# Three buffers for the split weights, modulation chunks in the mixers' room, an earlier first low half, and ten filler products for sixteen

## The reference, cut to what matters

```python
def swiglu(h, w_gate, w_up, w_down):
    return (jax.nn.silu(h @ w_gate) * (h @ w_up)) @ w_down
...
    cond = jax.nn.silu(c)
    for l in range(DEPTH):
        mod = (cond @ mod_w[l] + mod_b[l]).reshape(B, 9, D)
        h = modulate(rmsnorm_2(x, norm_g[l, 0]), mod[:, 0], mod[:, 1])
        x = x + 0.5 * mod[:, 2][:, None, :] * swiglu_2(h, ffn_w1[l, 0], ffn_w2[l, 0])
        h = modulate(rmsnorm_2(x, norm_g[l, 1]), mod[:, 3], mod[:, 4])
...
        x = x + mod[:, 5][:, None, :] * y
        h = modulate(rmsnorm_2(x, norm_g[l, 2]), mod[:, 6], mod[:, 7])
        x = x + 0.5 * mod[:, 8][:, None, :] * swiglu_2(h, ffn_w1[l, 1], ffn_w2[l, 1])
    return rmsnorm_2(x, final_norm_g)
```

## Time and profile before

| | us |
|---|---|
| median of 3 runs | 2264.15 (2263.81 to 2268.41) |
| the profiled execution, its own time | 2260.51 |
| its span in the trace | 2258.7 |
| PE busy in it | 2152.3 (95%) |
| DVE busy | 1611.8 (71%) |
| ACT busy | 1199.0 (53%) |

### The profile page before, as it was taken

How to read it: one execution, slowest core, us unless ns; L and a number is a source line. 1 busy time by engine, 2 the same in 40 slices (tenths; PEclk the granted TensorE clock), 3 DMA queues, 4 the chain that set the end, 5 groups by cost and what they waited for, 6 DMA issues and landing times.

```text
span 2258.7 us, 32271 instructions
## 1 busy us (share of the span) xinstructions
PE 2152.3 (95%) x12896; PEld 1852.2 (82%) x12896; DVE 1611.8 (71%) x2638; ACT 1199.0 (53%) x2024; POOL 41.8 (2%) x38
## 2 busy tenths in 40 slices
PE   8999978999999997999989999899999999999998
PEld 7888957888888895888878888688888888658887
DVE  7887486887787648688678767578776656786665
ACT  6554555554554455555465546555455544455553
POOL 0002000000001100000000000000000000000000
PEclk9999989999999998999999999899999999799999
DMA  7876412777577641277757764167755454103544
GB/s 271 290 262 224 167 56 88 257 254 247 208 262 263 224 164 46 103 260 245 258 176 260 241 222 148 61 208 260 239 188 186 174 197 137 69 1 131 186 170 147
DMA packets 78072, 426.29 MB, mean 189 GB/s; under 512 B 9696, under 2 KB 10464, under 8 KB 47632
## 3 DMA queue, kind: packets, MB, share of 16 engines
q1 hardware_dynamic: 77968, 424.95, 54.6%
HBM read 423.86 MB, written 1.05 MB: 188 GB/s over the span
## 4 chain that ended last, share of the span: by engine, by line
PE 73%; DVE 15%; DMA 6%; ACT 5%; issue 1%; DVEq 0%; ACTq 0%
PE bank L418 34%; PE bank L415 17%; DVE slot_lo L1162 6%; DMA slot<-in_wd_dram 5%; PE bank L408 4%; PE bank L410 4%; PE bank L409 4%; ACT slot_hi L848 2%; DMA slot<-in_slots_dram 2%; DVE h L1212 1%; PE bank L761 1%; PE bank L563 1%; PE bank L455 1%; DVE room L1434 1%; PE bank L475 1%
## 5 line engine op out<-in xcount | busy, mean ns | idle before, releaser
L1162 DVE TENSOR_TENSOR slot_lo<-slot,slot_hi 128x1024 fp32r<-128x1024 f32 (+1 forms) x728 | 799.2, 1113 | 279.2 <-ACT slot_hi L848 278.0
L418 PE MATMUL bank<-h_both,slot_hi 128*128 128x512 f32 x2816 | 970.6, 398 | 10.4 <-DVE slot_lo L1162 6.6
L848 ACT ACTIVATE slot_hi<-slot 128x1024 fp32r<-128x1024 f32 (+1 forms) x728 | 678.3, 957 | 268.0 <-PE bank L418 90.2
L415 PE MATMUL bank<-h_both,slot_lo 128*128 128x256 f32 x2816 | 734.3, 281 | 0.0
L418 PEld LDWEIGHTS bank<-h_both,slot_hi 128*128 128x128 f32 x2816 | 506.9, 188 | 111.2 <-issue 12.6
L415 PEld LDWEIGHTS bank<-h_both,slot_lo 128*128 128x128 f32 x2816 | 531.6, 189 | 31.7
L418 PE MATMUL bank<-act_both,slot_hi 128*128 128x512 f32 x1232 | 435.0, 398 | 5.9 <-DVE slot_lo L1162 5.7
L415 PE MATMUL bank<-act_both,slot_lo 128*128 128x256 f32 x1232 | 336.9, 281 | 0.0
L896 ACT ACTIVATE room<-bank 128x512 f32<-128x512 f32 x176 | 105.2, 598 | 351.2 <-PE bank L418 351.1
L418 PEld LDWEIGHTS bank<-act_both,slot_hi 128*128 128x128 f32 x1232 | 229.2, 188 | 61.8 <-DVE slot_lo L1162 9.3
L1262 DVE TENSOR_TENSOR room<-room,bank 128x512 f32<-128x512 f32 x176 | 121.1, 688 | 177.9 <-ACT room L896 177.9
(11 more groups left out here) (224 smaller groups left out, 2141.1 us busy)
## 6 DMA issues: line engine op xcount, KB each, us to landing
slot<-in_slots_dram SPq DMA_DIRECT2D x236, 1024.0 KB, 4.9
slot<-in_wd_dram SPq DMA_DIRECT2D x128, 704.0 KB, 4.2
mod_raw<-in_mod_w_dram SPq DMA_DIRECT2D x144, 512.0 KB, 5.2
room<-in_na_bias_dram SPq DMA_DIRECT2D x8, 512.0 KB, 5.6
x<-in_x_dram SPq DMA_DIRECT2D x1, 1024.0 KB, 4.9
out_dram<-h SPq DMA_DIRECT2D x4, 256.0 KB, 2.5
cond<-in_cond_dram SPq DMA_DIRECT2D x1, 512.0 KB, 9.3
lru_w<-in_lru_w_dram SPq DMA_DIRECT2D x1, 512.0 KB, 6.3
```

What stands on the lines that cost most here:

```text
L415: return pe.matmul(o[:, 0:S], slot_lo[b][:, w:w + P], x_both[:, 0, :], start=False, stop=False)
L418: end = pe.matmul(o, slot_hi[b][:, w:w + P], x_both.rearrange("p a b -> p (a b)"), start=first, stop=last)
L848: act.activation(slot_hi[b][:, c0:c1], slot[b][:, c0:c1], ACT.Copy).then_inc(s["hi_ready"], 1)
L1162: ins = dve.tensor_tensor(slot_lo[b][:, c0:c1], slot[b][:, c0:c1], slot_hi[b][:, c0:c1].bitcast(F32), ALU.subtract)
```

## The change

High and low parts get three buffers (`SPLIT_RING = 3`), the raw slots keep two. Splitting now runs one slot further ahead: two slots are split before the first norm, and each later place in ACT's and DVE's queues splits the slot after the one it split before. ACT's rounding of slot n so waits for PE to be done with slot n-3. The two `mod_raw` buffers move from memory of their own into `room`, memory that the mixers use, so that no modulation chunk can be loaded across a mixer: the first two loads of each FFN follow its slot 5, and `mod_chunk` stands in hidden steps 2 to 21 (20 of them) and in j = 0 to 3. In the norm the first low half stands behind two scaled chunks in place of three. `WARM` is 10 in place of 16 (the start keeps its 8 products). PE's hidden loop has three turns with six steps in the body, and its down phase is written out.

```diff
+SPLIT_RING = 3
...
 def mod_beside_hidden(c):
-    return c % 5 < 4
+    return c >= 2
...
-        slot_hi = [sb(f"slot_hi{i}", [P, SLOT], F32R) for i in range(RING)]
-        slot_lo = [sb(f"slot_lo{i}", [P, SLOT], F32R) for i in range(RING)]
-        mod_raw = [sb(f"mod_raw{i}", [P, D]) for i in range(2)]
+        slot_hi = [sb(f"slot_hi{i}", [P, SLOT], F32R) for i in range(SPLIT_RING)]
+        slot_lo = [sb(f"slot_lo{i}", [P, SLOT], F32R) for i in range(SPLIT_RING)]
...
+        mod_raw = [carve(at, D) for i in range(2)]
...
-        WARM = 16
+        WARM = 10
...
-            load_mod(0)
-            load_mod(1)
...
+                    if c == 5:
+                        load_mods(2)
+                    elif c > 5:
+                        load_mods(mod_beside_hidden(c - 5))
...
-                with loop(pe, seen, FC // 2 - 1, lo_ready=2, pair_read=2):
...
+                turns = (FC - 2) // (2 * SPLIT_RING)
+                with loop(pe, seen, turns, lo_ready=2 * SPLIT_RING, pair_read=2 * SPLIT_RING):
+                    for c in range(2 * SPLIT_RING):
+                        gate_up(c)
...
+            def split_hi_half(half):
+
+                n = seen.value("hi_split")
+                if n == len(SLOT_COLS):
+                    return
+                b, raw, cols = n % SPLIT_RING, n % RING, SLOT_COLS[n] // 2
...
-                lag = 2
-                for n in range(KC + lag):
...
+                raw(0)
+                raw(1)
+                low(0)
+                raw(2)
+                for n in range(3, KC):
+                    raw(n)
+                    low(n - 2)
+                low(KC - 2)
+                low(KC - 1)
+                split_both()
...
-            split_hi(0)
+            split_hi()
+            split_hi()
...
-            for _ in range(WARM // 2):
+            for _ in range(8):
```

More of the change, by code:

```diff
@@ L335, in load_ffn, with load_mods @@
             def load_ffn(n, ffn, first, bias=None):
-                chunk = ffn * MOD_GROUP + 2
+                chunk = ffn * MOD_GROUP
+                def load_mods(consumed):
+                    nonlocal chunk
+                    for _ in range(consumed):
+                        if chunk < (ffn + 1) * MOD_GROUP and ffn < MOD_GROUPS:
+                            load_mod(chunk)
+                            chunk += 1
                 for c in range(first, FC):
@@ L350, in load_ffn @@
                         load_down_slot((ffn * KC + j) * 2 + half)
-                        c, down = FC + 2 * j + half - 4, j - 2
-                        if ffn < MOD_GROUPS and (mod_beside_hidden(c) if c < FC else half == 1 and down < MOD_GROUP - MOD_BESIDE):
-                            load_mod(chunk)
-                            chunk += 1
+                        c = FC + 2 * j + half - 5
+                        load_mods(mod_beside_hidden(c) if c < FC else half == 0)
                     if bias is not None and 2 <= j < 6:
@@ L499, in down @@
                         last.then_inc(s["slot_done"], 1)
-                down(0)
-                down(1)
-                with loop(pe, seen, KC // 2 - 2, lo_ready=4, x_ready=2):
-                    down(2)
-                    down(3)
-                down(KC - 2)
-                down(KC - 1, narrow=True)
                 norm_sum(KC)
@@ L843, in link, with split_hi @@
                 act.wait_ge(s["act_step"], seen("act_step"))
-            def split_hi_half(b, half, cols):
-                c0, c1 = half * cols // 2, half * cols // 2 + cols // 2
-                act.activation(slot_hi[b][:, c0:c1], slot[b][:, c0:c1], ACT.Copy).then_inc(s["hi_ready"], 1)
-            def split_hi(b, cols=SLOT):
-                act.wait_ge(s[SLOT_READY[b]], seen(SLOT_READY[b], 16))
+            def split_hi_half(half):
[3 more added lines that the diff above has]
+                b, raw, cols = n % SPLIT_RING, n % RING, SLOT_COLS[n] // 2
+                if half == 0:
+                    act.wait_ge(s[SLOT_READY[raw]], seen(SLOT_READY[raw], 16))
+                else:
+                    seen("hi_split")
+                c0, c1 = half * cols, half * cols + cols
+                act.activation(slot_hi[b][:, c0:c1], slot[raw][:, c0:c1], ACT.Copy).then_inc(s["hi_ready"], 1)
+            def split_hi():
                 for half in range(2):
-                    split_hi_half(b, half, cols)
+                    split_hi_half(half)
             def rstd_of(target, sums, width, ready="rstd_ready"):
@@ L1156, in link, with split_lo, split_both @@
                 dve.wait_ge(s["dve_step"], seen("dve_step"))
-            def split_lo(b, part, cols=SLOT):
+            def split_lo(part):
+                n = seen.value("lo_split")
+                if n == len(SLOT_COLS):
+                    return
+                b, raw, cols = n % SPLIT_RING, n % RING, SLOT_COLS[n] // 2
                 dve.wait_ge(s["hi_ready"], seen("hi_ready"))
-                c0, c1 = ((0, cols // 2), (cols // 2, cols))[part]
-                ins = dve.tensor_tensor(slot_lo[b][:, c0:c1], slot[b][:, c0:c1], slot_hi[b][:, c0:c1].bitcast(F32), ALU.subtract)
+                c0, c1 = part * cols, part * cols + cols
+                ins = dve.tensor_tensor(slot_lo[b][:, c0:c1], slot[raw][:, c0:c1], slot_hi[b][:, c0:c1].bitcast(F32), ALU.subtract)
                 if part:
+                    seen("lo_split")
                     ins.then_inc(s["lo_ready"], 1)
-            def split_both(b, cols=SLOT):
-                split_lo(b, 0, cols)
-                split_lo(b, 1, cols)
+            def split_both():
+                split_lo(0)
+                split_lo(1)
             def add_squares(halves, n):
@@ L1225, in norm_of, with raw, low @@
-                split_both(1)
+                def raw(n):
+                    gain = mod_gain[:, layer, i, n:n + 1] if stack else gains[:, 3 * layer + i, n:n + 1]
+                    dve.scalar_tensor_tensor(out=h[:, n, :], in0=x[:, n, :], scalar=gain,
+                                             in1=rstd[:, :], op0=ALU.mult, op1=ALU.mult).then_inc(s["h_raw"], 1)
+                def low(k):
+                    dve.wait_ge(s["h_hi_ready"], seen("h_hi_ready"))
+                    hi = h_hi[:, k, :].bitcast(F32)
+                    if stack:
+                        c = (layer * 9 + 3 * i) * KC + k
+                        ins = dve.scalar_tensor_tensor(out=h_lo[:, k, :], in0=h[:, k, :], scalar=mod[:, c:c + 1],
+                                                       in1=hi, op0=ALU.add, op1=ALU.subtract)
+                    else:
+                        ins = dve.tensor_tensor(h_lo[:, k, :], h[:, k, :], hi, ALU.subtract)
+                    ins.then_inc(s["h_ready"], 1)
```

122 lines of the change are left out of this document (58 added, 64 removed).

## The result

The changed kernel takes 2241.57 us in the median of 16 runs (2232.72 to 2254.68), the kernel before beside it 2263.98 (16 runs): the ratio is 0.9902, with a 95% interval of 0.9879 to 0.9925, so it is 1.0% faster. I had said 2234 us, 1.3%. A later timing of the same kernel, six executions, gave 2236.36 us and 0.9897 (0.9871 to 0.9924).

What follows compares the result with a forecast made beforehand. PE's work was taken as the bound, with about 100 us idle to gain from: 8.5 + 18.2 + 3.0 - 1.6 = 28.1 us off 2260.5 gives 2232.4; half of the median's 3.6 added, 2234 us, range 2223 to 2250.

Steps and rivals of the forecast that it cites:

- the second stack's transitions: From `norm_sum`'s end to the second slot's end, five places: 1.8 us saved each, 9.0 us in all.
- the first stack's mixers: Transitions behind two mixers: 1.0 us from the start and 0.6 from the second slot each, 3.2 us in all.
- Down phase: FFN down products: a third buffer covers late slots and ends PE's stalls, 8.5 us saved (5.7 to 9.3).
- The third buffer's second slot: Behind a norm: the second slot is already split, so PE goes on without waiting; 0.6 us behind each first-stack mixer.
- The earlier start: Behind a norm: ten fillers and an earlier first low half let PE's products start 1.0 us earlier.
- Behind FFN 0, 1 and 2: Transitions with fillers at half clock: products start at T+3.85 in place of T+5.1, 1.25 us each, 3.75 us.
- Start and border: Kernel start and border of the stacks: 0.5 and 1.7 us saved, despite PE standing 1.6 and 1.3 us more.
- Ends of FFNs: `norm_sum`'s wait for the last square: fewer chunk loads in the down phase give 3.0 us back (0 to 7).
- Clock: Longer PE idle at start, border and transitions: a charge of 1.6 us (0 to 18) for half clock.
- the rival in which the clock falls behind every transition: Transitions with ten fillers: half clock costs 11 us at seven, 14 with two other places; 2247 us, chance 0.10.
- The larger loop: PE's hidden loop, six steps in the body: rival that each jump back stalls, 40 us, 2274 us; chance 0.06.

Runs made afterwards that it cites:

- buffers_mods: The changed kernel with sixteen fillers and the old order of the low halves, keeping the third buffer and the chunks' new places; 2236.56 us.
- before_warm10: The kernel before with ten fillers in place of sixteen, the start's eight kept; 2256.85 us.
- start_split1: The changed kernel with one slot split ahead of the first norm, as before, and the other behind it; 2235.97 us.
- border_fill: The changed kernel with 20 more filler products ahead of, and 8 behind, the `norm_sum` at the border of the stacks; 2233.87 us.
- low_lag1: The changed kernel with each low half right behind the next scaled chunk, not only the first; 2238.33 us.
- combined_hidden: The changed kernel with low halves at lag one, one slot split ahead of the first norm, border fillers, softplus series behind FFN 1's first hidden step; 2223.01 us.
- mods_late: The changed kernel with modulation chunks beside hidden steps from 4 on, not 2, so two more per FFN load in the down phase; 2237.87 us.
- warm4: The changed kernel with four fillers in place of ten; 2241.76 us.
- softplus_j4: The changed kernel with the softplus series behind piece 4 of FFN 1's down phase in place of piece 6; 2251.53 us.

## Why the prediction was nearly right

The total was nearer than its parts. Against the sum of 28.1 us the down phases, the ends and the transitions behind FFN 0, 1 and 2 gave 5.0 us more than predicted, and the second stack's transitions, the start, the border and the first stack's mixers 10.0 us less; that the one makes good half of the other is luck.

**Down phase: right.** 9.55 us against 8.5 (5.7 to 9.3 as its bounds); the stalls ended altogether, since all eight phases take the same 62.18 us. The row of the weight loads, 9.3 in the earlier trace rows, was the better guide.

**The third buffer's second slot: right in mechanism, and in the second stack it was the whole gain.** I had split 1.8 us per transition of the second stack into 1.0 for the earlier start and 0.8 for the slot. Measured are 1.15 (5.8 for five, where I had 9.0), and buffers_mods shows that sixteen fillers give them too: 15.98 to 14.91 us with the third buffer alone. In the kernel before, the same cut of fillers brought nothing where the clock was full (before_warm10). Behind the first stack's mixers I had 1.6 us each and 1.2 came: 0.7 for the slot, where I had 0.6, and 0.5 for the earlier start, where I had 1.0.

**The earlier start: the step that failed.** I took the last low half as the bound of the first slot: "it would want the eighth chunk at T+2.5+4.9 = T+7.4 and now waits for it; the first slot ends at T+8.4". The trace of FFN 5's end, after, says otherwise. DVE:

```profile
1647.87 0.48 DVE L1249 SCALAR_TENSOR_TENSOR h_both<-h,mod,h_both 128x256 fp32r<-128x256 f32 x1 [0.18 <-ACT h_both L906]
1648.28 0.87 DVE L1241 SCALAR_TENSOR_TENSOR h<-x,mod_gain,rstd 128x256 f32<-128x256 f32 x2
1649.07 0.48 DVE L1249 SCALAR_TENSOR_TENSOR h_both<-h,mod,h_both 128x256 fp32r<-128x256 f32 x1
...
1652.23 1.27 DVE L1249 SCALAR_TENSOR_TENSOR h_both<-h,mod,h_both 128x256 fp32r<-128x256 f32 x3
```

and PE:

```profile
1645.14 0.70 PE L485 MATMUL bank<-sq,ones 128*128 128x256 f32 x2 [0.59 <-ACT sq L938]
1645.49 2.67 PE L492 MATMUL bank<-slot_hi 128*128 128x512 f32 x10
1648.50 0.47 PE L435 MATMUL bank<-h_both,slot_hi 128*128 128x512 f32 x1 [0.34 <-DVE h_both L1249]
...
1649.60 0.50 PE L435 MATMUL bank<-h_both,slot_hi 128*128 128x512 f32 x1 [0.15 <-DVE h_both L1249]
...
1650.40 0.49 PE L435 MATMUL bank<-h_both,slot_hi 128*128 128x512 f32 x1
```

Here T is 1645.14 + 0.70 = 1645.84. Fillers' end, the first low half at T+2.5 and the last at T+7.7 are as I had them. But PE doesn't run freely up to the last chunk. The second low half ends at 1649.55, since the new order puts two scaled chunks ahead of it, and PE begins the second chunk at 1649.60, 0.4 us after it was ready to. From there it takes a chunk every 0.79 us, DVE's pace (1649.60, 1650.40, then on to the sixth chunk at 1652.78), not its own 0.70. The sixth chunk begins at T+6.9 with three chunks' products still to make; the first slot ends at T+9.3, not T+8.4, and at T+9.3 it had ended in the kernel before too. With a bound that follows each chunk rather than the last alone, the earlier start is worth almost nothing here, and the order of the low halves costs 0.2 to 0.3 us where I had given it 0.1 of gain.

**Behind FFN 0, 1 and 2:** 5.4 us against 3.75. I had left the half clock in place; but the end of FFN 0 no longer idles long (0.53 us for 2.16 in the earlier trace rows), and the fillers there run at full clock:

```profile
207.35 0.70 PE L485 MATMUL bank<-sq,ones 128*128 128x256 f32 x2 [0.53 <-ACT sq L938]
207.69 2.67 PE L492 MATMUL bank<-slot_hi 128*128 128x512 f32 x10
210.63 0.36 PE L425 MATMUL bank<-h_both,slot_hi 128*128 128x256 f32 x1 [0.27 <-DVE h_both L1252]
```

**Start and border: the sign was wrong.** I expected 2.2 us saved at the two, and lost 3.8. The two idle stretches were in the prediction (1.6 and 1.3 us more), but the price that I set, one stretch of 1.6 us for both at even odds, was too low: 3.4 to 10.2 us at half clock at each place. start_split1 and border_fill give 3.0 and 2.7 us back: at the border that shows idle time and the half clock behind it as the cause, at the start it is the half clock behind the longer idle time, 2.2 of the 3.0 us by low_lag1's start.

**Ends of FFNs:** the direction was right, and 5.3 us came where I took 3.0 (0 to 7). FFN 1's part was read from the sum of waits alone: its 2.8 us were mostly a late slot, but 25 small operations of DVE stood next in line, and once the slot was in time they held the end at 4.9 us. combined_hidden shows it: 1.66 us without them there. Elsewhere mods_late supports that loads moved out of the down phase are what helps, though to no better than 2 us.

**Clock:** I charged 1.6 us. The price at start and border stands above; the rival in which the clock falls behind every transition is refuted for ten fillers and comes about half true with four. In the mixers' inner part the change makes no difference that the runs' own variation would not cover.

**The larger loop: the rival fell.** The hidden phase is 112.80 us with a body of six steps, as it was with two, so no jump back costs anything that a row shows. The prediction let a rule of the Trainium skill (Runtime: NRT & Kernel Launch, Instruction fetch mechanics) speak against the body of 384 instructions: a taken branch outside two blocks of 16 KiB stalls for a fetch. The page gives each block 256 instructions, so two hold 512, and the body stalls by the rule only if the block behind the one that runs has left the memory when the branch comes. The prediction's "would stall" was firmer than that. The trace shows no stall; it fits the page's other figure, 2048 instructions for TensorE, and doesn't rule out the first.

## What to carry to other kernels

A third buffer for prepared weights pays where the consumer restarts: here 9.6 us in the stalling phases and 0.7 to 1.1 us at each norm with sixteen fillers. Fewer fillers give something on top only where the low halves keep ahead of PE (0.5 us at the first stack's mixers, nothing in the second stack), and without the buffer they become waits one slot later. A work item that the path doesn't need until later (the second slot's split, a series of tiny operations) belongs behind the work that it delays, and in the phase where its engine has room, not where it merely finds a gap. When two engines work through the same chunks in step, bound the consumer at every chunk and add what remains behind it; the last chunk alone gives a bound that is too early.

## What the runs showed of the hardware

Idle stretches of PE had different consequences by their length: 0.3 us ahead of a transition's first product left the clock at full where `norm_sum` hadn't waited long before, the 3.08 us at the start and 4.93 at the border brought 3.4 to 10 us at the lower level in the traces of after and of the experiments that keep them, but for one start (low_lag1, 3.09 us idle and no half clock), and 1.7 us (warm4) did so at some places and not at others. A chain of 25 dependent operations of DVE on 128x4 elements takes 4.8 us though each is busy for 0.16 to 0.18 us. In the last mixer the lower clock held for some 38 to 48 us in thirteen of the fourteen traces, and for 75 in one (softplus_j4), whose code there is that of after; this one place moves the time by up to 16 us, more than any of the edits tried but the whole change.
